# A hybrid attention and state-space step on one core: opening of the attention stage, border between scan and branches, and ninth tiles folded

## The reference

```
xn   = rmsnorm(x, norm1_w);   proj = xn @ w_in        # q k v f z xbc dt g_att g_ssm
q, k = rmsnorm per head;      logf = log_sigmoid(f + b_f)
att  = softmax(q k' / 8 + c_q - c_k, causal) @ v      # c = running sum of logf, 16 heads of 64
xbc  = silu(causal_conv(xbc));  y = ssd(x, dt, A, B, C, h0) + D * x
y    = grouped_rmsnorm(y * silu(z)) * ssm_norm_w
merged = sigmoid(g_att) * (att @ w_pa) + sigmoid(g_ssm) * (y @ w_pb)
x    = x + merged @ w_out
x    = x + relu(rmsnorm(x) @ w_up)**2 @ w_down
```

## Time and profile before

| | |
|---|---|
| median of 3 runs | 2943.19 us |
| the profiled execution | 2946.99 us, of which the span of instructions is 2945.2 us |
| busy share of the span | PE 96%, DVE 55%, ACT 31%, POOL 9% |
| mean granted clock of PE | 0.976 of full speed |
| `norm_split` and the head of the program | 0 to 41 us |
| `project_qkv` | 41 to 388 us |
| attention stage | 388 to 1357 us |
| scan | 1357 to 1734 us |
| branches | 1734 to 2061 us |
| `out_norm` | 2061 to 2191 us |
| `mlp` | 2191 to 2945 us |

### The profile page before, as it was taken

How to read it: one execution, slowest core, us unless ns; L and a number is a source line. 1 busy time by engine, 2 the same in 40 slices (tenths; PEclk the granted TensorE clock), 3 DMA queues, 4 the chain that set the end, 5 groups by cost and what they waited for, 6 DMA issues and landing times. The chain is left out here.

```text
span 2945.2 us, 49177 instructions
## 1 busy us (share of the span) xinstructions
PE 2815.1 (96%) x19530; PEld 2740.2 (93%) x19530; DVE 1630.6 (55%) x3155; ACT 903.2 (31%) x2161; POOL 250.9 (9%) x379
## 2 busy tenths in 40 slices
PE   6998979999999999998999979999889999999999
PEld 6998969999999999997999969999889999999999
DVE  4235237666676576675888973643364444344444
ACT  4223324444444444443343331220331111111110
POOL 0000000000000000001555530000000000000000
PEclk8999989999999999999999989999999999999999
DMA  3222222232221322324888861342331111111112
GB/s 113 88 88 53 76 74 76 71 91 70 76 90 50 91 76 71 89 68 116 194 201 202 192 190 68 118 136 76 110 117 44 44 44 57 45 44 44 43 69 93
DMA packets 335636, 269.07 MB, mean 91 GB/s; under 512 B 111440, under 2 KB 311760, under 8 KB 335280
## 3 DMA queue, kind: packets, MB, share of 16 engines
q1 hardware_dynamic: 335408, 265.93, 31.2%
HBM read 193.58 MB, written 72.28 MB: 90 GB/s over the span
## 5 line engine op out<-in xcount | busy, mean ns | idle before, releaser
L379 PE MATMUL banks<-w_hi,xn_hi 128*128 128x256 f32 x1440 | 413.7, 287 | 7.1 <-DVEq L337 4.7
L379 PE MATMUL banks<-w_lo,xn_hi 128*128 128x256 f32 x1440 | 411.0, 285 | 0.0
L379 PE MATMUL banks<-w_hi,xn_lo 128*128 128x256 f32 x1440 | 410.4, 285 | 0.0
L382 PE MATMUL banks<-xn_hi,w_hi 128*128 128x352 f32 x1152 | 377.7, 328 | 0.0
L382 PE MATMUL banks<-xn_hi,w_lo 128*128 128x352 f32 x1152 | 375.8, 326 | 0.0
L382 PE MATMUL banks<-xn_lo,w_hi 128*128 128x352 f32 x1152 | 375.6, 326 | 0.0
L379 PEld LDWEIGHTS banks<-w_hi,xn_hi 128*128 128x128 f32 x1440 | 277.6, 193 | 9.2 <-DVEq L337 4.8
L379 PEld LDWEIGHTS banks<-w_lo,xn_hi 128*128 128x128 f32 x1440 | 276.0, 192 | 0.6
L379 PEld LDWEIGHTS banks<-w_hi,xn_lo 128*128 128x128 f32 x1440 | 275.9, 192 | 0.0
L1623 PE MATMUL banks<-h_hi,w_hi 128*128 128x352 f32 x768 | 248.7, 324 | 1.9 <-DVEq L1544 1.9
L1623 PE MATMUL banks<-mlp_uhi,w_hi 128*128 128x352 f32 x768 | 248.5, 324 | 0.0
(11 more groups left out here) (277 smaller groups left out, 6225.8 us busy)
## 6 DMA issues: line engine op xcount, KB each, us to landing
w_raw<-in_w_in SPq DMA_DIRECT2D x44, 1024.0 KB, 5.6
scratch_xbc<-att_co SPq DMA_DIRECT2D x32, 512.0 KB, 2.6
ssd_ab<-scratch_acum SPq DMA_DIRECT2D x64, 256.0 KB, 6.0
scratch_gates<-ssd_tanh SPq DMA_DIRECT2D x48, 176.0 KB, 5.5
br_g<-scratch_gates SPq DMA_DIRECT2D x48, 176.0 KB, 2.5
scratch_z<-att_z_stage SPq DMA_DIRECT2D x64, 128.0 KB, 2.4
ssd_xbc<-scratch_xbc SPq DMA_DIRECT2D x64, 128.0 KB, 3.3
ssd_xbc<-scratch_xbc SPq DMA_DIRECT2D x128, 64.0 KB, 3.7
```

Source lines behind the costliest of these rows:

```text
L379: ins = self.nc.tensor.matmul(self.bank(n, P, PW), x[:, k, t * P:(t + 1) * P], w[:, k, :], start=first, stop=end)
L382: ins = self.nc.tensor.matmul(self.bank(n, P, TT), w[:, k, m * P:(m + 1) * P], x[:, k, r * TT:(r + 1) * TT], start=first, stop=end)
```

## The change

1. **Ninth tiles folded.** The columns behind the running frames in the high part (`T` to `T+32`) no longer hold zeros but a copy of the low part of the running frames. The ninth tile is then 16 matmuls (high by high, high by low), whose rows 32 to 63 hold the low part's product, and DVE adds them to rows 0 to 31 (`fold`, two operations) before anyone reads the bank.
2. **Attention opens with two tiles.** `FIRST` = 2 tiles of the stream are multiplied before the first scores, and the tiles without a step are spread anew over the remaining 166.
3. **Order of SP's first loads.** `start_sp` (convolution rows, panel) comes before the loads of head 0.
4. **Border of scan and branches.** The last gate tile is multiplied whole behind the scan. Three row buffers, the norm weights' buffer, Y, the states' and the gates' buffers outlive the scan (`Handover`). The first three row tiles are loaded in the scan's last 9 steps. The waits for stores move to where the data is used. `branches` begins with attention and `w_pa`, whose rows need no scaling, and `rms` is finished there.
5. `MergeFm` follows that order (the first four panels take one DVE operation per tile, the others two, as before in number; 72 gate loads in place of 48). `SiluTm.RING` is 2 in place of 3.

```diff
@@ norm_split, DVE (the same in out_norm)
-            nc.vector.memset(hi[:, :, T:TW].bitcast(F32), 0.0).then_inc(padded, 1)
-            nc.vector.memset(lo[:, :, T:TW].bitcast(F32), 0.0).then_inc(padded, 1)
+            nc.vector.memset(hi[:, :, T + TS:TW].bitcast(F32), 0.0).then_inc(padded, 1)
...
+            dve.wait_ge(lo_made, 2 * (NT + 1))
+            nc.vector.tensor_copy(hi[:, :, T:T + TS], lo[:, :, TP:T].bitcast(F32)).then_inc(padded, 1)
@@ Stream
     def wait_full(self, eng, i, n):
         eng.wait_ge(self.full, i * self.slots + n + 1)
+        if n in self.running:
+            eng.wait_ge(self.folded, i * len(self.running) + self.running.index(n) + 1)
+
+    def fold(self, dve, i, n):
+        if n not in self.running:
+            return
+        dve.wait_ge(self.full, i * self.slots + n + 1)
...
+        self.nc.vector.tensor_copy(self.under[:], bank[TS:2 * TS, :]).then_inc(self.lifted, 1)
+        dve.wait_ge(self.lifted, u + 1)
+        self.nc.vector.tensor_tensor(bank[0:TS, :], bank[0:TS, :], self.under[:], ALU.add).then_inc(self.folded, 1)
@@ Stream.pe_part
-        passes = [(x, w, k) for k in range(KB) for x, w in ((self.hi, wh), (self.hi, wl), (self.lo, wh))]
+        factors = ((self.hi, wh), (self.hi, wl)) if n in self.running else ((self.hi, wh), (self.hi, wl), (self.lo, wh))
+        passes = [(x, w, k) for k in range(KB) for x, w in factors]
@@ attention_z_xbc
-        every = total // (total - E)
-        steps = [None if n % every == every - 1 else order[n - n // every] for n in range(total)]
+        FIRST = 2
+        rest, alone = total - FIRST, total - FIRST - E
+        steps = [None] * FIRST
+        left = iter(order)
+        for n in range(rest):
+            steps.append(None if (n + 1) * alone // rest > n * alone // rest else next(left))
@@ ssd_gates, SP and PE
+                if e >= E - 9 and e % 3 == 0:
+                    handed.load_rows(sp, (e - (E - 9)) // 3)
...
-            gates.finish(sp)
-            for j in range(YR):
-                sp.wait_ge(y_stored[j], 16 * (E // YR))
-            sp.wait_ge(st_stored, 32 * G)
+            stream.sp(sp, *LAST, True)
...
             turn_out(G - 1)
+            stream.pe(pe, *LAST)
@@ branches, SP
+                if u == ST:
+                    handed.wait_y(sp)
+                sp.wait_ge(turned, 2 * (u - 2))
+                handed.load_rows(sp, u)
+            stream.load(sp, 0, 1)
+            for u in range(handed.ROWS, HEAD + 2):
                 load_rows(u)
-            stream.load(sp, 0, 1)
+            handed.wait_gates(sp)
+            for n in range(2):
+                merge.load_gate(sp, n)
+            handed.load_weights(sp)
+            handed.wait_states(sp)
```

More of the change, by code:

```diff
@@ L277, in __init__ @@
         self.by_range = False
+        self.running = [n for n, (j, t) in enumerate(self.tiles) if panels[j][0] and t == NT]
+        if self.running:
+            self.under = sb(f"{tag}_under", [TS, PW])
+            self.lifted, self.folded = sem(f"{tag}_lifted"), sem(f"{tag}_folded")
     def mine(self, ep, n):
@@ L1243, in _ @@
                 make_hi(u)
+            act.wait_ge(meaned, 1)
+            nc.scalar.activation(rms[:], rms[:], ACT.Sqrt).then_inc(rooted, 1)
             for n in range(stream.slots):
@@ L1886, in _ @@
                 prep(0, g)
-            for n in range(total):
+            for n in range(FIRST, total):
                 i, j, _ = tile(n)
```

171 lines of the change are left out of this document (100 added, 71 removed).

## The result

The changed kernel takes 2891.95 us (median of 4 runs, 2890.95 to 2892.78), the kernel before 2943.39 us on the same chip (2942.64 to 2944.92). The ratio is 0.9824, with a 95% interval from 0.9807 to 0.9841: 51.4 us less, where 50.0 were forecast.

A forecast was written before the change was run, and what follows sets the result against it. TensorE (PE), busy 96% of the span, was taken as the bound. Terms 16.7 - 0.4 + 17.3 + 3.4 + 13.0 = 50.0 us off 2943.2 gave 2893 us, range 2880 to 2908 (8 in 10).

The forecast's parts named there:

- Folds: Ninth tiles in qkv, attention and out_norm: 8 matmuls dropped in each of 24 tiles; 16.7 us, less 0.4 for a copy.
- Alignment of head loads: Attention: panel loads no longer queue behind the next head's loads, removing seven stalls and low clock; 17.3 us.
- I give the seven 13.0 us: Attention: share of PE's 14.0 us of waits assigned to the seven stalls behind head loads.
- The clock's 6.3 us: Attention: time saved when 85 matmuls run at 2.4 GHz in place of 1.2 GHz after four stalls; 6.3 us.
- the 2.0 us for new coincidences: Attention: loss as drifting steps of much DVE work meet such tiles; -2 us, bounds 0 and -8.
- Opening: Start of attention: convolution rows issued first, loop 4.5 us later but two tiles (7.9 us) done; gain 3.4 us.
- Border: Scan to branches: first product starts earlier, 14.3 us less 1.3 for low clock; gain 13.0 us, bounds 9 and 17.
- the 12 us by the rule: Border gain if transposes don't raise the clock and the first product starts at 1.2 GHz: nearer 12 us than 13.
- New coincidences: Rival, attention: other stalls of like size replace the seven, alignment gains nothing; 2910 us, chance 0.13.
- Matmuls not on the path: Rival, attention and out_norm: the epilogue sets the pace, folds give 4 us in place of 16.3; 2905 us, chance 0.08.
- Two-buffer z ring: Rival "Slower": ACT held at some 70 z tiles until stores land, 140 us more; 3033 us, chance 0.02.
- The change doesn't do what it says: Rival: key loads behind the panel delay PE at the opening; opening and border give a third; 2904 us, chance 0.08.

The follow-up runs named there:

- open-order kernel: Changed kernel with the second keys' high and low parts made ahead of the exponential and v's splitting in the attention opening: 2887.71 us.
- kernel with the rows first: Changed kernel with the fourth and fifth row tiles requested ahead of the 1 MB panel load at the scan/branches border: 2891.65 us.

## Why the prediction was right, step by step

The total held: 50.0 us forecast, 51.4 measured; 2893 against 2891.95. The four parts, each undone or made alone, give 14.4 to 17.9 (forecast 16.3), 21.6 (17.3), 3.8 (3.4) and 10.2 us (13.0): between 50.0 and 53.5 in all. So within their intervals of some 4 us each they add. That the total is right to 1.4 us is in part luck: the second part was too small and the fourth too large, and the two errors cancel.

- **Folds.** Right in size, place and in the tiles that save nothing. In attention the folds gave 7.0 us and the way to the scan took 0.8 back: 6.2 us, where 8 x 0.96 - 0.96 - 0.7 = 6.0 were counted.
- **Alignment of head loads.** The mechanism was right and is shown in both directions; the term was too small, by 4.3 us against the edit made on the kernel before (21.6), by 1.2 if the six coincidences brought back are scaled to seven (18.5). The reading "I give the seven 13.0 us" was right: their waits are 0.9 to 3.0 us and sum to 12.7. But a wait is listed from a modelled end of the matmul before, and by the distances of the starts 15.7 us of stalls went from the stage. The clock's 6.3 us were 7.2. And the 2.0 us for new coincidences didn't come: two waits of 0.6 us stand in the whole loop, with DVE busy for 66% as before.
- **Opening.** Right in its steps, its size not settled (3.8 to 6.8 us): transposes 10.2 us behind the last qkv matmul (9 said), loop 3.3 us later (4.5 said). The missed step is the exponential and `split_v` ahead of the second keys, of which the forecast had only the bank copies: a wait of 4.8 us, which the open-order kernel takes half away.
- **Border.** From the last gate matmul to the first product 12.7 us, as forecast (12 to 14). The error lies in front of it: "the last scan step ends some 3 us earlier on PE, and the whole gate tile (24 x 0.165 = 4.0 us) follows" was to put the last gate matmul 0.9 us later than PE's last work before, and it came 3.65 later, reckoned from the scan's start. PE's last transposes came 1.6 us earlier than before (361.3 against 362.9), not 3, and the tile ended 5.4 us behind them (1688.96 to 1694.33), not 4.0: from 1688.7 to 1692.1 PE ran at 1.2 GHz. Each makes 1.4 us of the miss. The fall comes again in run after run. In eight of the nine kernels that multiply this tile whole behind the scan, PE waited 1.2 to 1.8 us in the last step, and 3.4 or 6.8 us at 1.2 GHz came with it. In the ninth, the one without folds, it waited under 0.8 us, the clock stayed at 2.4 GHz and the tile was as short as forecast (3.8 us). In the five with the fillers in their places there is neither wait nor fall before the scan's end. So the fillers had covered these waits, a term that the forecast put at nothing; what exactly makes the clock fall isn't shown. The 1.3 us for a longer low clock at the first product did not come. By the stage of the kernel with the old border the miss is only 0.5 us (12.5 against 13.0), so its size is open.
- **Clock at the transposes.** The Trainium skill, "TensorE: Matmul & The Clock Gate", Part 4 (PE-mode transpose), says that transposes don't count as activity. The traces don't agree. In the changed kernel 24 of them ran with 2.4 GHz granted (1696.7 to 1700.1), and the clock fell only after 2.3 us of idle PE. And it also rises from them alone, which the trace of before already held: its timeline of PE, its window up to the one that the forecast used, and a window of the kernel with the rows first:

```profile
1749.12 3.67 PE L1222 MATMUL banks<-ident,br_rows 128*128 128x128 f32 x16 [14.85 <-DVE br_rows L1260]
```

```profile
1749.12:1753.20 4.08, 3.67 (x16) 3.26 (x16) 3.67 (x9) 2.16 (x4) 0.00 (x0) 0.51 0.28 87
...
1699.40:1702.80 3.40, 3.40 (x17) 3.40 (x18) 1.54 (x3) 1.79 (x3) 0.00 (x0) 0.51 0.23 39
```

After 14.9 us of idle PE there were 16 transposes at 1.2 GHz and nothing else, and at 1753.2 the clock went to 2.4. In the kernel with the rows first it rose at 1702.8, behind 17 transposes at 1.2 GHz. So keeping the row was right; that the 12 us by the rule lie nearer to the 10.2 measured is chance, since the first product ran at 1.2 GHz for as long as before (2.1 us).
- **Rivals.** New coincidences: none. Matmuls not on the path: no. Two-buffer z ring: no wait of ACT for a store of z is listed, and the folds' kernel carried the ring at no price that can be seen. Of the signs named beforehand, all came, three of them with another size: the convolution transposes 10.2 us behind the last qkv matmul in place of 9; the qkv stage shorter by 9.95 us against 8 to 9, within what qkv spreads between profiles of like code (334.7 to 336.5); `out_norm` with the way to the MLP by 1.5 against 2. In the rival "The change doesn't do what it says", the fourth tile's time is mis-added too (1736.6 + 5.6 + 4.8 is 1747.0, not 1746.5), and the sum itself counts the start of the second load twice, as the landings show.

## What to carry to other kernels

When a periodic table of steps meets a periodic stream of loads, list where two bursts fall on one slot of the issuing queue: one transfer put ahead of eight small ones was worth at least as much here as 192 matmuls. Price a stall by the distances between starts and add the low clock behind it; a wait that only shrinks may keep its low clock, one that goes takes it along. Don't add two times from issue to landing: take one of them and the distance between landings. When work is pulled together at the end of a stage, look at what it covered there and at which clock it will run.

## What had not been expected of the hardware

- Each of the seven stalls cost 3.1 us of kernel time, though its wait is listed with 1.8 us in the mean (0.9 to 3.0). Most of the rest was time at 1.2 GHz: four windows of 17.1 us in all, 7.2 us more than the same matmuls take at 2.4 GHz. The kernel before had them behind the first, third, fifth and sixth stall, the one with folds alone behind the second, fifth and sixth: not every stall brings one, and the length doesn't decide alone (before, the one with 2.54 us between two starts brought none, the one with 1.65 us did).
- A 512 KB row tile issued 0.6 us behind a 1 MB panel was used 5.9 us after issue, one issued ahead of it after 3.7. It landed after the panel, in both traces 1.3 us behind it, so the order was kept and only 2.2 us were lost.
- PE ran 24 transposes in 3.4 us with 2.4 GHz granted, and the clock fell in the idle time after them. Twice it rose from 1.2 to 2.4 GHz behind 16 or 17 transposes with no other matmul between.
